# Hybrid decoder trunk, two layers: the first two column blocks side by side, squares later, rope steps every 13 ticks

## The reference

```python
xn = rms_norm(h, norm_g)
proj = xn @ w_in
...
qh = rope(rms_norm(qb.reshape(b, p, HB, DH_B), q_norm_g), pos)
kh = rope(rms_norm(kb.reshape(b, p, KVH_B, DH_B), k_norm_g), pos)
vh = vb.reshape(b, p, KVH_B, DH_B)
yb = swa_sink_attention(qh, kh, vh, sinks).astype(h.dtype)
...
mixed = jnp.concatenate([ya * jax.nn.silu(ga), yb * jax.nn.silu(gb),
                         yc * jax.nn.silu(gc)], axis=-1)
return h + mixed @ w_out
```

## Time and profile before

| | |
|---|---|
| time, median of 3 runs | 1594.33 us (1594.26 to 1594.99) |
| the profiled execution's own time | 1594.23 us |
| its span | 1592.4 us |
| granted clock of PE, mean | 0.999 |
| PE busy | 1562.3 us, 98% |
| DVE busy | 912.8 us, 57% |
| ACT busy | 669.9 us, 42% |
| POOL busy | 172.9 us, 11% |

### The profile page before, as it was taken

One profiled execution on the slowest core, in us unless ns is written; L12 is line 12 of the kernel. 1 busy time (PEld: TensorE's weight loads), 2 busy tenths in 40 slices (PEclk: granted clock), 3 DMA queues, 4 the chain that ended last, 5 costly groups with the idle time before them and its releaser, 6 DMA issues.

```text
span 1592.4 us, 26784 instructions
## 1 busy us (share of the span) xinstructions
PE 1562.3 (98%) x10732; PEld 1440.5 (90%) x10732; DVE 912.8 (57%) x1737; ACT 669.9 (42%) x1320; POOL 172.9 (11%) x312
## 2 busy tenths in 40 slices
PE   6999999999999999999999999999999999999999
PEld 6999899999999999999998889888989888888887
DVE  7676687666566544334345776776675564433231
ACT  7777566613322423223236775665132333322121
POOL 0000665400000000000000006543000000000000
PEclk9999999999999999999999999999999999999999
DMA  6222111214112223334342231111321212334341
GB/s 253 89 96 91 54 54 58 73 62 113 72 54 80 80 80 113 128 124 158 121 147 83 79 107 54 62 72 54 107 80 57 77 64 95 106 107 159 122 157 67
DMA packets 38299, 151.70 MB, mean 95 GB/s; under 512 B 5264, under 2 KB 13984, under 8 KB 22944
## 3 DMA queue, kind: packets, MB, share of 16 engines
q1 hardware_dynamic: 38176, 150.00, 27.7%
HBM read 141.13 MB, written 8.59 MB: 94 GB/s over the span
## 4 chain that ended last, share of the span: by engine, by line
PE 92%; DVE 4%; issue 1%; POOL 1%; ACT 0%; DMA 0%; SPq 0%; DVEq 0%; POOLq 0%
PE ps_gemm L942 80%; PE ps_mix L867 3%; PE ps_mix L789 2%; PE ps_mix L835 2%; PE ps_mix L803 1%; PE ps_gemm L764 1%; DVE rstd L1027 1%; PE ps_mix L911 1%; PE ps_mix L831 1%; DVE w_lo L1009 1%; PE ps_mix L913 0%; POOL w_lo L470 0%; PE ps_mix L900 0%; PE ps_mix L862 0%; DMA w_stage<-in_w_in 0%
## 5 line engine op out<-in xcount | busy, mean ns | idle before, releaser
L942 PE MATMUL ps_gemm<-x_hi,w_hi 128*128 128x264 f32 (+1 forms) x2240 | 560.4, 315 | 13.7 <-DVE w_lo L1009 10.6
L942 PE MATMUL ps_gemm<-x_hi,w_lo 128*128 128x264 f32 (+1 forms) x2240 | 542.4, 307 | 0.0
L942 PE MATMUL ps_gemm<-x_lo,w_hi 128*128 128x264 f32 (+1 forms) x2240 | 542.0, 307 | 0.0
L942 PEld LDWEIGHTS ps_gemm<-x_hi,w_hi 128*128 128x128 f32 x2240 | 363.7, 189 | 35.6 <-DVE w_lo L1009 11.3
L942 PEld LDWEIGHTS ps_gemm<-x_hi,w_lo 128*128 128x128 f32 x2240 | 363.1, 189 | 19.4
L942 PEld LDWEIGHTS ps_gemm<-x_lo,w_hi 128*128 128x128 f32 x2240 | 362.7, 189 | 16.6
L555 ACT ACTIVATE w_hi<-w_stage 128x512 fp32r<-128x512 f32 x464 | 266.3, 619 | 160.9 <-DVE z L1089 122.7
L1009 DVE TENSOR_TENSOR w_lo<-w_stage,w_hi 128x512 fp32r<-128x512 f32 x392 | 256.6, 689 | 75.6 <-ACT w_hi L555 65.2
L942 PE MATMUL ps_gemm<-mixed_hi,w_lo 128*128 128x264 f32 (+1 forms) x768 | 205.3, 322 | 0.0
L942 PE MATMUL ps_gemm<-mixed_lo,w_hi 128*128 128x264 f32 (+1 forms) x768 | 205.0, 321 | 0.0
L942 PE MATMUL ps_gemm<-mixed_hi,w_hi 128*128 128x264 f32 (+1 forms) x768 | 203.8, 320 | 0.0
(11 more groups left out here) (178 smaller groups left out, 1522.9 us busy)
## 6 DMA issues: line engine op xcount, KB each, us to landing
w_stage<-in_w_in SPq DMA_DIRECT2D x83, 1024.0 KB, 4.8
w_stage<-in_w_out SPq DMA_DIRECT2D x32, 1024.0 KB, 5.1
x_in<-in_xT SPq DMA_DIRECT2D x4, 1056.0 KB, 9.9
res<-in_xT SPq DMA_DIRECT2D x16, 264.0 KB, 5.2
h1T<-z SPq DMA_DIRECT2D x16, 264.0 KB, 5.5
res<-h1T SPq DMA_DIRECT2D x16, 264.0 KB, 5.2
a_rden<-rden SPq DMA_DIRECT2D x32, 128.0 KB, 4.9
out<-z SPq DMA_DIRECT2D x16, 256.0 KB, 5.5
```

Of the source, the lines that this page charges most:

```text
L942: ins = pe.matmul(g[:, bank, 0:size], ws, xs[:, k, c:c + size], start=tick == 0 and i == 0, stop=tick == TICKS - 1 and i == 2)
```

## The change

1. **Blocks 0 and 1 side by side.** For each chunk k, PE does a step (six matmuls) of block 0 and one of block 1; block 1 skips four turns and does its last four chunks at the end. x arrives in six pieces of 1, 1, 2, 4, 4, 4 chunks instead of four of 4; the parameters and the first two weight quarters of block 1 are sent from ACT's queue. ACT and DVE split both blocks' weights among the x chunks. Two matmuls over zeros (line 867) stand ahead of the first block.
2. **Evicted raw.** ACT copies blocks 0 and 1 out of PSUM without rstd (raw_out, line 616), and DVE multiplies z by rstd in place later (line 1227). PE starts blocks 2 and 3 on the raw copy.
3. **Squares.** Four are made among the first chunks, twelve in block 2, with w_hi and w_lo of blocks 2 and 3 between them. The rstd mini moves to tick 4 of block 3, the V transposes to tick 8 of block 3.
4. **Rope steps of layer 0** begin at tick 8 of block 3 and then every 13 ticks (minis go to two banks of M); rope_last stands 13 ticks behind a step's beginning. Blocks 0 to 5 are taken out at ticks of their own (LATE_OUT, counted from the layer's start). In layer 1 all of these stay at the ticks of before.
5. The differences of the lower bounds, the masks and the coefficients move to blocks 2, 5 and 6; the rope table is sent behind the last square, V's meta rows from slot 3 on.

The core of the diff:

```diff
+
+RMS_AT = (3 * TICKS + 4, 1 * TICKS + 11)
+ROPE_AT = ([3 * TICKS + 8 + 13 * r for r in range(9)], [TICKS * (2 + r) for r in range(9)])
+ROPE_LAST = (13, 17)
+LATE_OUT = {0: 3 * TICKS + 6, 1: 3 * TICKS + 6, 2: 62, 3: 72, 4: 84, 5: 98}, {0: 1 * TICKS + 12}
+V_AT = (3 * TICKS + 8, 2 * TICKS + 1)
+
+
+def rope_at(layer, n, tick, after):
+
+    at = TICKS * n + tick - after
+    return ROPE_AT[layer].index(at) if at in ROPE_AT[layer] else None
+
+
+def chunks_out(N, tick):
+
+    layer, n = divmod(N, len(IN_CHUNKS) + KC)
+    if tick == 0 and N and not (n and n - 1 in LATE_OUT[layer]):
+        yield N - 1
+    for c in LATE_OUT[layer]:
+        if LATE_OUT[layer][c] == TICKS * n + tick:
+            yield N - n + c
...
+
+X_PIECES = ((0, 1), (1, 2), (2, 4), (4, 8), (8, 12), (12, 16))
+EARLY_SQUARES = {3: 0, 6: 1, 9: 2, 12: 3}
+N_EARLY = len(EARLY_SQUARES)
+SECOND_SKIPS = (3, 7, 11, 15)
+WARM_MATMULS = 2
+SECOND_HI = {1: (2, 2), 4: (2, 3), 6: (3, 0), 8: (3, 1), 10: (3, 2), 12: (3, 3)}
...
-            sp.dma_start(prm_sb[:], prm).then_inc(s_prm0, 16)
+            def load_x(i):
+                ks = slice(*X_PIECES[i])
+                sp.dma_start(xin[:, ks], xT[:, ks]).then_inc(s_x[i], 16)
+
+            def load_first_w(c, k0, k1, done):
+                sp.dma_start(wst[:, c, k0:k1].rearrange("p k c -> p (k c)"), w_in[0, c, :, k0 * P:k1 * P])\
+                  .then_inc(done, 16)
+
             load_x(0)
-            sp.dma_start(wst[:, 0, 0:4].rearrange("p k c -> p (k c)"), w_in[0, 0, :, 0:4 * P]).then_inc(s_wfirst, 16)
+            load_first_w(0, 0, 4, s_wq[0][0])
             load_x(1)
-            sp.dma_start(wst[:, 0, 4:].rearrange("p k c -> p (k c)"), w_in[0, 0, :, 4 * P:]).then_inc(s_w[0], 16)
             load_x(2)
+            load_first_w(0, 4, 8, s_wq[0][1])
             load_x(3)
-            load_w(1)
-            sp.dma_start(pw_sb[:].rearrange("p l g c -> p l (g c)"), pool_w).then_inc(s_prm, 16)
-            sp.dma_start(cst[:], c_f32).then_inc(s_prm, 16)
-            sp.dma_start(cst2[:], c_mask).then_inc(s_prm, 16)
...
             for N in range(NTOT):
                 layer, n = divmod(N, NC)
...
-                if n == 0:
+                if N == 0:
+                    sp.dma_start(pw_sb[:].rearrange("p l g c -> p l (g c)"), pool_w).then_inc(s_prm, 16)
+                    sp.dma_start(cst[:], c_f32).then_inc(s_prm, 16)
...
+                if n == (0 if layer else 2):
 
                     sp.wait_ge(s_xlo, 16)
                     sp.wait_ge(s_xsq, 16)
                     if layer:
...
-                if n == 2:
...
+            for c, q in ((1, 0), (1, 1)):
...
+                              w_in[0, c, :, 4 * q * P:4 * (q + 1) * P]).then_inc(s_wq[c][q], 16)
...
-            act.wait_ge(s_lb, 1)
-            act.activation(lbt[:, 2:4], lbt[:, 0:2], ACT.Exp).then_inc(s_lb, 1)
             for k in range(KC):
-                if k % 4 == 0:
-                    act.wait_ge(s_x[k // 4], 16)
+                for i, (k0, _) in enumerate(X_PIECES):
+                    if k == k0:
+                        act.wait_ge(s_x[i], 16)
                 x_high(0, k, xin[:, k])
...
-                if k % 4 == 0:
-                    w_high(0, k // 4)
+                if k == 0:
+                    w_high(0, 0)
+                    w_high(1, 0)
+                if k % 4 == 2 and k < 12:
+                    w_high(0, k // 4 + 1)
+                if k % 4 == 3 and k < 12:
+                    w_high(1, k // 4 + 1)
+                if k in EARLY_SQUARES:
+                    x_square(0, EARLY_SQUARES[k], xin[:, EARLY_SQUARES[k]])
...
+                    if N == 1 and tick == 0:
+                        w_high(2, 0)
+                        raw_out(0)
+                        w_high(2, 1)
+                    if N == 2:
+                        if tick == 0:
+                            raw_out(1)
+                        if tick < KC - N_EARLY:
+                            x_square(0, N_EARLY + tick, xin[:, N_EARLY + tick])
+                        if tick in SECOND_HI:
+                            w_high(*SECOND_HI[tick])
...
+            def first_blocks():
+
+                def step(c, k):
+                    if k % 4 == 0:
+                        pe.wait_ge(s_wlo, 2 * (k // 4) + c + 1)
+                    if c == 0:
+                        pe.wait_ge(s_xlo, k + 1)
+                    for i, (ws, xs) in enumerate(((wh[:, c, k], xh), (wh[:, c, k], xl), (wl[:, c, k], xh))):
+                        for bank, c0, size in parts(0, T // 2):
+                            ins = pe.matmul(G[:, c, bank, 0:size], ws, xs[:, k, c0:c0 + size],
+                                            start=k == 0 and i == 0, stop=k == KC - 1 and i == 2)
+                    if k == KC - 1:
+                        ins.then_inc(s_gemm, 1)
+
+                pe.wait_ge(s_zero, 1)
+                for _ in range(WARM_MATMULS):
+                    pe.matmul(M[:, 3], z[:, 0, 0:P], z[:, 0, 0:512], start=True, stop=True)
+                second = 0
+                for k in range(KC):
+                    step(0, k)
+                    if k not in SECOND_SKIPS:
+                        step(1, second)
+                        second += 1
+                for k in range(second, KC):
+                    step(1, k)
...
+                if N < 2:
+                    continue
+                if N < 4:
+                    pe.wait_ge(s_raw, N - 1)
+                else:
                     pe.wait_ge(s_z, N - 1)
...
+                    if TICKS * n + tick == RMS_AT[layer]:
+                        if layer == 0:
+                            pe.wait_ge(s_prm, 48)
+                        mini(N, layer, 1)
+                    r = rope_at(layer, n, tick, MINI_TICK)
+                    if r is not None:
+                        mini(N, layer, 2 + r)
+                    if slot_minis(n) and tick == mini_tick(n):
                         mini(N, layer, n)
...
+                    if TICKS * n + tick == V_AT[layer]:
+
+                        pe.wait_ge(s_z, NC * layer + 1)
...
-                if k % 4 == 0:
-                    w_low(0, k // 4)
-                if 1 <= k <= EARLY_SQUARES:
-                    x_sum(0, k - 1)
+                if k == 0:
+                    w_low(0, 0)
+                    w_low(1, 0)
+                if k % 4 == 2 and k < 12:
+                    w_low(0, k // 4 + 1)
+                if k % 4 == 3 and k < 12:
+                    w_low(1, k // 4 + 1)
+                if k in EARLY_SQUARES:
+                    x_sum(0, EARLY_SQUARES[k])
...
+                if N < 2:
+                    dve.wait_ge(s_raw, N + 1)
+                    signal(dve.tensor_tensor(zz, zz, rstd[:], ALU.mult), s_z)
+                    return
...
-                    if tick == (RMS_TICK + 1 if n == 1 else 0) and N:
-                        take_out(N - 1)
-                    if N == 0 and tick == 13:
-                        for k in range(EARLY_SQUARES, KC):
-                            x_sum(0, k)
+                    r = rope_at(layer, n, tick, ROPE_LAST[layer])
+                    if r is not None and layer == 0:
+                        rope_last(r + 1)
+                    for out in chunks_out(N, tick):
+                        take_out(out)
+                    if N == 1 and tick == 0:
+                        w_low(2, 0)
+                        w_low(2, 1)
+                    if N == 2:
+                        if tick < KC - N_EARLY:
+                            x_sum(0, N_EARLY + tick)
+                        if tick in SECOND_HI:
+                            w_low(*SECOND_HI[tick])
...
+                    if N == 2 and tick == 9:
+                        lb_differences()
...
+                    r = rope_at(layer, n, tick, 2)
...
-                    if N == 4 and tick == 7:
+                        square_low(norm_no(layer, 2 + r), sql[:, c], ta_[:, c], sqh[:, c])
+                    if N == 5 and tick == 7:
                         level_masks()
-                    if N == 3 and tick == 7:
+                    if N == 6 and tick == 7:
                         hgrn_coefficients()
-                    if tick == 1 and N >= 2 and CHUNKS[(N - 2) % NC][0] in ("k", "q"):
-                        rope_last(N - 2)
+                    r = rope_at(layer, n, tick, ROPE_LAST[layer])
+                    if r is not None and layer:
+                        rope_last(NC * layer + r + 1)
```

173 lines of the change are left out of this document (99 added, 74 removed).

## The result

| | before | changed |
|---|---|---|
| median | 1594.30 us (1593.11 to 1594.99, 6 runs) | 1600.52 us (1599.48 to 1601.46, 6 runs) |
| profiled execution's own time | 1594.23 us | 1600.59 us |
| span | 1592.4 us | 1598.8 us |
| granted clock of PE, mean | 0.999 | 0.996 |

The ratio is 1.0042, 95% interval 1.0033 to 1.0052: slower by 6.2 us. The first blocks did end 9.5 us sooner, and all of that and more was lost behind them.

What follows compares the result with a forecast made beforehand. PE, busy 98%, was taken as the bound. Start 32.6, work 110.7 and waits 12.7 put block 11 at 156.0, +3.0 us; a 1.4 us clock fall made +4.4, forecast 1598.6 us, range 1592.0 to 1602.5.

Steps and rivals of the forecast that it cites:

- the sign: Whole kernel: slower was given 0.55, same 0.33 and faster 0.12.
- Start: Blocks 0 and 1: first step at 7.7 us, and the first two blocks end (E) at 32.6.
- The term of 1.5 us for a slow clock: First matmul pairs: seven run 0.44 us apart instead of 0.25, costing 1.5 us (bounds 0 and 1.5).
- Rival D: Start: x comes late or ACT's sends and table load hold x_hi; E 3 us later, 1601.6 us; chance 0.10.
- Squares and V: Block 3: statistics mini almost without wait (0.1 us), then PE waits 1.1 us for z at the V transposes.
- The eviction of block 2: Ahead of block 4: z stands behind V's low parts, square_low and rope_first; PE waits 5.8 us (4.5 to 6.5).
- The rope steps: Minis of steps 2, 3 and 4: PE waits 0.85, 0.4 and 4.4 us for square_low, none later.
- The clock: Behind the long waits: one new fall, 1.4 us, after block 4's 5.8 us wait, none after the 4.4 us wait.
- rival C: Behind the 4.4 us wait: a second clock fall, 1.5 us more, 1600.1 us; chance 0.15.
- rival B: Waits as costed, no clock fall in the 5.8 us wait, warm-up matmuls work; 1595.7 us, no change; chance 0.30.
- The sum: E to block 11: 110.7 us of PE work and 12.65 of waits; block 11 at 156.0 against 153.03.
- What stays: From block 11 on, layer 1 included: same work in the same slots, minis' bank moves cost nothing.

Runs made afterwards that it cites:

- e7: The changed kernel with ACT's table load put ahead of its wait for the first piece of x; 1600.88 us, ratio 1.0046.
- e12: The changed kernel with block 2 evicted at tick 58, coefficients in block 0, x's fourth piece split, layer 0's minis one tick later, three warm-up matmuls; 1591.45 us.
- e1: The changed kernel with block 2 taken out at tick 58 instead of 62, ahead of square_low and the first rotation; 1595.37 us, ratio 1.0007.
- e4: The changed kernel with filler matmuls keeping PE at work, 24 ahead of block 4's wait and 17 ahead of step 4's mini; 1599.17 us, ratio 1.0031.
- e2: The changed kernel with level masks moved from block 5 to 9 and HGRN coefficients from block 6 to 10; 1599.59 us, ratio 1.0036.
- e3: The changed kernel with block 2 taken out at tick 58, level masks in block 9 and coefficients in block 10; 1593.72 us, ratio 0.9998.
- e5: The changed kernel without its two warm-up matmuls; 1601.34 us, ratio 1.0047.
- e9: The changed kernel with x's fourth piece, chunks 4 to 7, sent as two pieces of two chunks; 1600.32 us, ratio 1.0043.

## Why the prediction was right, point by point

The time, 1600.5, lies in the range, and the sign was the one given 0.55; the forecast of 1598.6 was 1.9 low.

- **Start.** The first step came at 7.59 (7.7 forecast), E at 32.73 (32.6). That agreement is luck in part. The term of 1.5 us for a slow clock was wrong in this execution: the earlier trace rows had slow pairs behind 9.0 us of nothing, and here the first pairs ran at full speed behind two warm-up matmuls, which took 3.8 us and not 1.7. In its place x came late, 1.12 us at chunk 4 and some small delays. The prediction compared the landing of x's fourth piece (12) with PE's need (14). It was there at 12.68, its first chunk took 1.7 us more through x_hi and x_lo, and PE at full clock had come at 13.25. In the change and all twelve experiments block 2 started between 32.73 and 33.71. Where the first pairs were all fast (the change, e7, e12), PE's waits for x add up to 1.1 to 1.6 us; where pairs were slow, to 0.4 or nothing. The two take each other's place. That x alone sets the start is not shown, since in the executions with slow pairs PE was at work nearly throughout. (The 19 us given for DVE's work is 19.4 by its own prices, which changes nothing.) Rival D had the mechanism, with a size far too large.
- **Squares and V.** The mini at 48.06 (forecast 48.0); the wait for V 0.62 (1.1).
- **The eviction of block 2**, the step that was said to decide: z was out at 63.79, 31.1 behind E (31.5 forecast), PE had come 25.4 behind E (25.7), and it waited 5.68 (5.8). The sum of measured rows in the new order was right to 0.4 us, and e1 shows that the order is the cause: one row moved, and 4.7 of the 5.7 are gone.
- **The rope steps.** 1.01, 0.28 and 4.14 (0.85, 0.4 and 4.4), and none at steps 5 to 8, as said. At step 4 this is a difference that came out better than its two sides: square_lo was done 48.3 us behind block 4's start (46.4 forecast), and PE had come at 44.3 (42.0). The fall of the clock made PE later, and DVE's chain was longer than its sum: in e4, without a fall, square_lo was done at 47.2. (The 7.1 us given for three w_lo, square_low, z, y and rope_first is 7.2 by the prediction's own prices.) Where e2 and e3 were expected to gain all of it, the same sum was not made again for the new places of the load.
- **The clock.** That the second wait would have no fall was the step that failed: "5.8 is nearer to 9.0, 4.4 to 2.1, so I take one new fall, 1.4 us, and not a second". It fell, and cost 2.7. This is rival C, given 0.15 and priced at 1.5. By the Trainium skill, page "TensorE: Matmul & The Clock Gate", section "HAM oscillation — how this bites in real kernels", each such wait is followed by slow matmuls; both long waits of this trace agree with it. The prediction's ground, that in the kernel before a wait of 2.1 us left the clock alone and only 9.0 us did not, left out a row of the same trace: the pairs behind the 1.83 us at 407.49 are slow. That "the clock column never leaves 1.00", rival B's argument, is wrong for the same stretch (0.91). The first fall cost 1.4 us, as taken, in this execution. In e2, e5, e7 and e9, behind the same 5.7 us, the stretch from block 4 to step 1's mini took 13.2 to 13.5 us (12.35 in the change, 10.95 with the filler), so it cost 2.2 to 2.6: the agreement is luck in part. PE then waited at step 2 for 0.2 us or nothing instead of 1.01. The second fall's slow stretch was about 6 us long in the change and about 3 in e1, behind the same wait, so the size of a fall could not be read from one case.
- **The sum.** It gave block 11 at 156.0 and with the fall 157.4; it started at 155.07+0.49+5.12 = 160.7. Of the 3.3 us, 2.7 are the second fall; the terms above take back 0.7 (E +0.1, V -0.5, block 4 -0.1, steps -0.2). Some 1.3 are left. The rows show where most of it is: a wait of 0.28 at 97.91 stands behind a pair that started at 97.23, 0.68 before it where 0.25 is usual. PE's end is modelled, so the idle time in the bracket leaves out about 0.15, and the next pair starts 0.33 behind it instead of 0.25. Five waits from E on, at some 0.2 each, make 1.0 of it; 0.3 is not placed.
- **What stays.** From block 11 on nothing changed, except for the fall at 400 to 420 that the profile of before has and this one lacks. It hid 1.4 of the 7.8, and so brought the forecast from 3.3 us low to 1.9 low: luck, since the prediction had no term for it.

## What to carry to other kernels

When work is packed closer, write out the new order of the engine that serves the bottleneck and add up measured durations along it: the wait at block 4 was forecast to 0.1 us in this way, and its two ends to 0.4. Then look for the one row that could stand ahead of others (an eviction that frees a bank goes before work that nobody waits for yet), and for gaps earlier, not later, to put small work into; here these two edits made a change that lost 6.2 us into one that gains 2.0. Time saved ahead of a loop that another engine sets was mostly waited away in it: with both edits block 2 started 9 us sooner, and 2 to 2.5 were kept.
